# Three-term query products from the second head on, one-hots that read their numbers from PSUM in groups of four tokens, and ten dots a head

## The reference

```
q = (h @ w_q).reshape(B, S, 8 heads, 2, 128)              # query
s = einsum(q, keys)                                       # 128 scores per half, head and token
s_top, i_top = top_k(s, 16)                               # per half
cand = s_top[..., 0, :, None] + s_top[..., 1, None, :]    # 256 candidates
best, pos = top_k(cand, 16); gate = softmax(best)         # 16 experts per head and token
act = gelu(u_tab[idx] . h)                                # idx out of 128*128 experts
y   = sum over the 8*16 experts of gate * act * v_tab[idx]
```

## Time and profile before

| | |
|---|---|
| median of three runs | 3626.38 us |
| the profiled execution itself | 3628.21 us, its span 3626.4 us |
| PE busy | 3406.7 us (94%) |
| DVE busy | 2795.2 us (77%) |
| POOL busy | 1892.1 us (52%) |
| ACT busy | 1113.5 us (31%) |
| mean DMA rate | 236 GB/s |

### The profile page before, as it was taken

The page is one execution under the profiler, slowest core; times in us unless marked ns, Lnnn a source line. Parts: engine busy times, 40 slices in busy tenths (PEclk is TensorE's granted clock), DMA queues, the critical chain, the costliest instruction groups (busy, mean ns, idle before and its releaser), DMA issues. The chain is left out here.

```text
span 3626.4 us, 53931 instructions
## 1 busy us (share of the span) xinstructions
PE 3406.7 (94%) x20084; PEld 2774.6 (77%) x20084; DVE 2795.2 (77%) x4779; ACT 1113.5 (31%) x1630; POOL 1892.1 (52%) x1128
## 2 busy tenths in 40 slices
PE   5998999889999999999999959899999999999995
PEld 2444888748889999988888834688899998888884
DVE  6672455447999999678888864599999994898987
ACT  0112434212223433333333301222243333333332
POOL 1210000015667666678888700456676657888883
PEclk9988999799999999999999979999999999999998
DMA  7750000036778778799999930577788879999994
GB/s 282 280 186 25 2 2 2 12 149 219 277 277 284 226 263 276 278 365 337 340 342 340 315 122 0 181 258 284 261 262 269 265 240 368 341 337 349 340 337 146
DMA packets 366847, 856.06 MB, mean 236 GB/s; under 512 B 32681, under 2 KB 201105, under 8 KB 358322
## 3 DMA queue, kind: packets, MB, share of 16 engines
q1 hardware_dynamic: 281394, 542.91, 44.2%
q0 software_dynamic: 85248, 310.42, 23.7%
HBM read 750.40 MB, written 102.81 MB: 235 GB/s over the span
## 5 line engine op out<-in xcount | busy, mean ns | idle before, releaser
L1442 PE MATMUL peer_acc<-peer_hhi,peer_uhi 128*128 128x384 f32 x2048 | 703.7, 344 | 7.8 <-POOL peer1same_ulo L1607 4.0
L1442 PE MATMUL peer_acc<-peer_hlo,peer_uhi 128*128 128x384 f32 x2048 | 687.2, 336 | 0.0
L1607 POOL TENSOR_TENSOR peer1same_ulo<-peer_u,peer_uhi 128x1024 fp32r<-128x1024 f32 x128 | 337.5, 2638 | 235.0 <-ACT peer_uhi L1510 232.2
L1607 POOL TENSOR_TENSOR peer0same_ulo<-peer_u,peer_uhi 128x1024 fp32r<-128x1024 f32 x128 | 338.0, 2643 | 233.5 <-ACT peer_uhi L1510 231.2
L1442 PEld LDWEIGHTS peer_acc<-peer_hhi,peer_uhi 128*128 128x128 f32 x2048 | 386.8, 189 | 13.2 <-POOL peer1same_ulo L1607 4.8
L1442 PEld LDWEIGHTS peer_acc<-peer_hlo,peer_uhi 128*128 128x128 f32 x2048 | 386.8, 189 | 3.8 <-issue 3.8
L1629 POOL TENSOR_TENSOR peer1lsame_vlo<-peer1l_v,peer1l_vhi 128x1024 fp32r<-128x1024 f32 x128 | 313.3, 2448 | 83.3 <-ACT peer1l_vhi L1535 81.2
L1629 POOL TENSOR_TENSOR peer0lsame_vlo<-peer0l_v,peer0l_vhi 128x1024 fp32r<-128x1024 f32 x128 | 312.6, 2442 | 84.7 <-ACT peer0l_vhi L1535 82.3
L1506 ACT ACTIVATE peer_gel<-peer_acc 128x384 f32<-128x384 f32 x256 | 125.7, 491 | 745.6 <-PE peer_acc L1442 714.4
L1657 DVE SCALAR_TENSOR_TENSOR peer_acc<-peer_row,peer_p_g,peer_acc 128x1024 f32<-128x1024 f32 x254 | 324.8, 1279 | 35.6 <-DMA peer_row<-in_pe_v,peer_idx 33.1
L1442 PE MATMUL peer_acc<-peer_hhi,peer0same_ulo 128*128 128x384 f32 x1024 | 343.8, 336 | 0.0
(11 more groups left out here) (357 smaller groups left out, 7081.9 us busy)
## 6 DMA issues: line engine op xcount, KB each, us to landing
peer_u<-in_pe_uT SPq DMA_DIRECT2D x256, 512.0 KB
peer0l_v<-in_pe_v SPq DMA_DIRECT2D x128, 512.0 KB
peer1l_v<-in_pe_v SPq DMA_DIRECT2D x128, 512.0 KB
activations<-peer_gel SPq DMA_DIRECT2D x256, 192.0 KB
rw_g<-in_ada POOLq DMA_DIRECT2D x80, 512.0 KB, 5.2
routing<-peer0m_wb SPq DMA_DIRECT2D x24, 1024.0 KB, 8.2
peer0l_wt<-routing SPq DMA_DIRECT2D x64, 384.0 KB
peer0l_gl<-activations SPq DMA_DIRECT2D x128, 192.0 KB
```

Of the source, the lines that this page charges most:

```text
L1442: mm = pe.matmul(ub[e % 2][:, 0:SD], a, h[:, k], start=(n == 0), stop=(n == 3 * KT - 1))
L1607: g.tensor_tensor(ulo[:, q].rearrange("p k e -> p (k e)"), u[:, q].rearrange("p k e -> p (k e)"), uhi[:, e % NH].bitcast(F32).rearrange("p ...
```

## The change

1. `query(n)` for n > 0 is a three-term product of 24 matmuls per half: whi*hhi + whi*hlo + wlo*hhi. The weights of head n + 1 are rounded by ACT in two instructions of 1024 elements a partition (`round_query`), in its steps 7n + 2 and 7n + 4, behind `tile_step`. POOL subtracts in two instructions (`low_query`), in its steps 7n + 3 and 7n + 5, behind `low_u` and ahead of the fetches. `whi` lies over `hT`, `wlo` over `wq`. `hhi` and `hlo` are made for 512 columns where there were 384.
2. The list of numbers 0 to 127 (`iota`) is copied to PSUM once, and the one-hots read it there. Groups are of 4 tokens (G = 4), two for each of the 48 tiles; each has its own waits and its own ACT copy.
3. HEAD_DOTS is 10. The 12 dots of a layer that this takes from six heads go to the blocks (57 there, where there were 45).
4. Buffers are laid elsewhere: `pf`, `hot_i` and the rows of the last layer norm.

```diff
-HEAD_DOTS = 12
+HEAD_DOTS = 10
...
-        G = 8
+        G = 4
         GROUPS = P // G
+        A_TILE = GROUPS // BLOCK_TILES
...
+        whi, wlo = over("whi", [P, 2, KT, 2 * P], F32R), over("wlo", [P, 2, KT, 2 * P], F32R)
...
+        iota_p = four[3][:, 0:P]
...
                 def query(n):
                     pe.wait_ge(w_loaded[n % 2], 32 * (n // 2) + 32)
+                    if n > 0:
+                        pe.wait_ge(wlo_made, 2 * n)
                     for s in range(2):
+                        cs = slice(s * P, (s + 1) * P)
                         if n > 0:
                             pe.wait_ge(q_taken, 2 * n + (s - 1))
                         for k in range(KT):
-                            mm = pe.matmul(qb[s], wq[:, n % 2, k, s * P:(s + 1) * P], hT[:, k], start=(k == 0), stop=(k == KT - 1))
+                            if n == 0:
+                                mm = pe.matmul(qb[s], wq[:, 0, k, cs], hT[:, k], start=(k == 0), stop=(k == KT - 1))
+                            else:
+                                pe.matmul(qb[s], whi[:, n % 2, k, cs], hhi[:, k], start=(k == 0), stop=False)
+                                pe.matmul(qb[s], whi[:, n % 2, k, cs], hlo[:, k], start=False, stop=False)
+                                mm = pe.matmul(qb[s], wlo[:, n % 2, k, cs], hhi[:, k], start=False, stop=(k == KT - 1))
                         mm.then_inc(q_done, 1)
...
                     if AT_BLOCKS <= e < AT_LAST:
-                        spread_group(e - AT_BLOCKS)
+                        for n in range(A_TILE * (e - AT_BLOCKS), A_TILE * (e - AT_BLOCKS + 1)):
+                            spread_group(n)
...
+                def round_query(n, half):
+                    ks = slice(half * KT // 2, (half + 1) * KT // 2)
+                    if half == 0:
+                        act.wait_ge(w_loaded[n % 2], 32 * (n // 2) + 32)
+                        act.wait_ge(q_done, 2 * n)
+                        if n <= 2:
+                            act.wait_ge(hlo_made, KT)
+                    a.activation(whi[:, n % 2, ks].rearrange("p k e -> p (k e)"), wq[:, n % 2, ks].rearrange("p k e -> p (k e)"),
+                                 ACT.Copy).then_inc(whi_made, 1)
...
                     tile_step(e)
                     if n < HEADS and r == 0:
                         take_scores(n)
+                    if n + 1 < HEADS and r in (2, 4):
+                        round_query(n + 1, r // 2 - 1)
...
+                def low_query(n, half):
+                    ks = slice(half * KT // 2, (half + 1) * KT // 2)
+                    pool.wait_ge(whi_made, 2 * (n - 1) + (half + 1))
+                    g.tensor_tensor(wlo[:, n % 2, ks].rearrange("p k e -> p (k e)"), wq[:, n % 2, ks].rearrange("p k e -> p (k e)"),
+                                    whi[:, n % 2, ks].bitcast(F32).rearrange("p k e -> p (k e)"), ALU.subtract).then_inc(wlo_made, 1)
...
                 for e in range(ET):
                     low_u(e)
+                    n, r = divmod(e - 1, HEAD_TILES)
+                    if 0 <= n < HEADS - 1 and r in (2, 4):
+                        low_query(n + 1, r // 2 - 1)
                     if e >= HEAD_TILES + 2:
...
-                iota = const["iota"][:]
+                v.tensor_copy(iota_p, const["iota"][:]).then_inc(iota_made, 1)
+                dve.wait_ge(iota_made, 1)
                 dve.wait_ge(slotT_made, 3)
                 for n in range(DT * GROUPS):
                     if n >= 2:
                         dve.wait_ge(spread_done, n - 1)
-                    v.tensor_tensor(hot_j[n % 2], iota.unsqueeze(1).to_broadcast([P, G, P]), spread(slotT[:, 2, n * G:(n + 1) * G], P),
+                    v.tensor_tensor(hot_j[n % 2], iota_p.unsqueeze(1).to_broadcast([P, G, P]), spread(slotT[:, 2, n * G:(n + 1) * G], P),
                                     ALU.is_equal).then_inc(j_made, 1)
                     for q in range(n * G, (n + 1) * G):
-                        ins = v.tensor_scalar(hot_i[:, n % 2, q % G], iota, slotT[:, 1, q:q + 1], slotT[:, 0, q:q + 1], ALU.is_equal,
+                        ins = v.tensor_scalar(hot_i[:, n % 2, q % G], iota_p, slotT[:, 1, q:q + 1], slotT[:, 0, q:q + 1], ALU.is_equal,
                                               ALU.mult)
                     ins.then_inc(i_made, 1)
```

More of the change, by code:

```diff
@@ L1034, in _ @@
             if load_norm is not None:
[L1035 removed]
+                load_norm(sp, rows_loaded, kept)
             if x is not None:
@@ L1277, in phase_peer @@
         gate_g, p_g = arena("gate_g", [P, SLOTS]), arena("p_g", [P, SLOTS])
-        same = Arena(nc, arena.prefix + "same", arena.offset, arena.end)
+        same, ending = Arena(nc, arena.prefix + "same", arena.offset, arena.end), Arena(nc, arena.prefix + "n", arena.offset, arena.end)
+        norm = dict(x=x_sb, **{n: ending(n, [P, D]) for n in ("gate", "g_row", "b_row")})
         u, ulo = arena("u", [P, NU, KT, P]), same("ulo", [P, NU, KT, P], F32R)
@@ L1283, in phase_peer @@
         early = Arena(nc, arena.prefix + "a", shared, arena.end)
+        over = Arena(nc, arena.prefix + "aover", shared, arena.end)
         hT, wq = early("hT", [P, KT, S]), early("wq", [P, 2, KT, 2 * P])
+        whi, wlo = over("whi", [P, 2, KT, 2 * P], F32R), over("wlo", [P, 2, KT, 2 * P], F32R)
         keyT, qT = early("keyT", [P, 2, 2, P]), early("qT", [P, 2, 2, S])
@@ L1299, in phase_peer @@
         wb = middle("wb", [P, 2, P, P // 2])
-        hot_i = middle("hot_i", [P, 2, G, P])
-        hot_j = [kept[n][:].rearrange("p (g q) -> p g q", q=P) for n in ("gate", "g_row")]
+        hot_i = kept["b_row"][:].rearrange("p (b g q) -> p b g q", b=2, q=P)
+        hot_j = [kept[n][:, 0:G * P].rearrange("p (g q) -> p g q", q=P) for n in ("gate", "g_row")]
         late = Arena(nc, arena.prefix + "l", shared, arena.end)
@@ L1307, in phase_peer @@
         vhi = late("vhi", [P, NH, D], F32R)
-        phi, plo, pf = late("phi", [P, NH, SD], F32R), late("plo", [P, NH, SD], F32R), late("pf", [P, NH, SD])
+        phi, plo = late("phi", [P, NH, SD], F32R), late("plo", [P, NH, SD], F32R)
+        pf = [kept[n][:, 0:SD] for n in ("gate", "g_row", "b_row")]
+        assert len(pf) == NH
         acc = ctx.enter_context(nc.psum_tensor(f"{name}_acc", [P, TT, D], F32))
@@ L1314, in phase_peer @@
         qb, sb = four[0:2], [b.rearrange("p (t k) -> p t k", k=P) for b in four[2:4]]
-        hb = [acc[:, b].rearrange("p (t i) -> p t i", i=P) for b in range(2)]
+        hb = [b.rearrange("p (t i) -> p t i", i=P) for b in four[0:2]]
+        iota_p = four[3][:, 0:P]
         x_turned, h_made, hhi_made, hlo_made = sem("x_turned"), sem("h_made"), sem("hhi"), sem("hlo")
@@ L1324, in phase_peer @@
         uhi_made, ulo_made, act_done, gel_made = sem("uhi"), sem("ulo"), sem("act_done"), sem("gel")
+        whi_made, wlo_made, iota_made = sem("whi"), sem("wlo"), sem("iota")
         j_made, i_made, spread_done, taken = sem("hot_j"), sem("hot_i"), sem("spread"), sem("taken")
@@ L1563, in _ @@
                     if AT_BLOCKS <= e < AT_LAST:
-                        take_group(e - AT_BLOCKS)
+                        for q in range(A_TILE * (e - AT_BLOCKS), A_TILE * (e - AT_BLOCKS + 1)):
+                            take_group(q)
                     if e == AT_LAST:
@@ L1758, in _ @@
                     n_rows += 1
+                dve.wait_ge(spread_done, DT * GROUPS)
                 weigh(0)
@@ L1768, in _ @@
                 assert n_dots[0] == n_rows == SLOTS
-        phase_mixer_out(nc, const, Arena(nc, arena.prefix + "o", shared, arena.end), kept, name + "o", y_rows=acc, out=dst)
+        phase_mixer_out(nc, const, Arena(nc, arena.prefix + "o", shared, arena.end), norm, name + "o", y_rows=acc, out=dst)
 def hybrid_trunk(nc, x, xT, ada, ln_g, ln_b, cols_in, const_in, heads_in, scan_in, rw_w_rkv, rw_w0, rw_w1, rw_w2, rw_a1, rw_a2,
@@ L1805, in hybrid_trunk @@
     kept = dict(x=keep("x", [P, TT, D]), **{n: keep(n, [P, D]) for n in ("gate", "g_row", "b_row")})
-    norm_loads = lambda layer, which: lambda sp, loaded: load_norm_rows(sp, kept, layer, which, mod_rows, ln_g[layer, which],
-                                                                        ln_b[layer, which], loaded)
+    norm_loads = lambda layer, which: lambda sp, loaded, into: load_norm_rows(sp, into, layer, which, mod_rows, ln_g[layer, which],
+                                                                              ln_b[layer, which], loaded)
     phase_mixer_out(nc, const, late("out0", rwa.offset), kept, "out0", y_rows=rw["g"], w_out=rw_w_o[0], x=x,
@@ L1811, in hybrid_trunk @@
     pea = late("peer", fixed.offset)
-    pe_t = dict(hhi=pea("hhi", [P, KT, S - P], F32R), hlo=pea("hlo", [P, KT, S - P], F32R))
+    pe_t = dict(hhi=pea("hhi", [P, KT, S], F32R), hlo=pea("hlo", [P, KT, S], F32R))
     E = pe_v.shape[0] // DEPTH
```

24 lines of the change are left out of this document (12 added, 12 removed).

## The result

The changed kernel takes 3735.5 us (median of 4 runs, 3731.9 to 3739.1) against 3627.0 us for the kernel before (4 runs): ratio 1.030 [1.028, 1.033], so 3.0% slower. Its profiled execution took 3731.85 us with a span of 3729.8 us, 103.4 us more than the span of before.

The account below looks back on a forecast made before the run. PE was taken to set the heads and V stage, with DVE next and 7.6 us of the blocks lost to something else. 3628.2 - 39.8 (queries) + 131.4 (stalls) + 78.4 (clock) - 35 (one-hots) = 3763 us; range 3675 to 3815.

Parts of the forecast that it names:

- Queries: Heads: half a query as 48 fp32r matmuls takes 10.89 us against 13.73 a head; -39.8 us over 7 heads, 2 layers.
- The stalls: Heads: `low_query` waits for `whi` in POOL's queue, `ulo` comes late, PE idles 3.4 to 5.7 us; +131.4 us.
- rival 4: Stalls in the heads: DVE keeps the shared port and holds POOL up; +20 us, 3783, counted in the forecast's range.
- The clock: Heads, behind each of 28 stalls: PE's clock falls to 1.2 GHz, costing 2.8 us each; +78.4 us.
- Rival 1: Heads: the stalls come without the clock's fall, heads of 52 us; 3685 us, chance 0.10.
- Blocks: Blocks: one-hots reading PSUM no longer wait for POOL, tiles of 6.0 us; -35 us for two layers.
- Errata and port: Blocks: by the skill's cycle costs a PSUM one-hot is 131 ns dearer, 0.39 us, DVE's tile 5.7 us, still PE's.
- Rivals 2 and 3: 2: POOL's lead covers the wait, 3553 us, chance 0.11; 3: blocks' one-hots still wait for POOL, 3798 us, chance 0.07.
- Costs taken as nothing: `hhi`/`hlo` for 512 columns, moved buffers, waits on `spread_done` and `iota_made`, half-size ACT copies: no cost counted.
- Ten dots: Heads: DVE's 43.09 us less 2 dots of 1.14 is 40.8, under the shorter head's 41.9.

Follow-up runs that it names:

- the fourth experiment: The changed kernel with 24 extra, unused matmuls of 384 columns ahead of PE's waits for `ulo` of tiles 7n+4 and 7n+6: 3683.1 us, ratio 1.017.
- eighth experiment: The best version (both roundings earlier, 3540.8 us) with the first v-table rows fetched at most two a step from POOL's step 115: 3543.8 us, ratio 0.979.

## Why the prediction was right, step by step

The forecast was 3763 us, 0.7% above the 3735.5 measured.

- **Queries.** Said -39.8. The last interval of each head went from 17.89 to 15.11 us: 2.78 each, -39.0 for 14.
- **The stalls.** Said 14 a layer, 131.4 us, behind tiles 7n + 3 and 7n + 5. Measured 14 a layer, 133.6 us. Heads 2 to 6 were said to have 5.7 and 4.5 and had 5.65 and 4.41; head 1, 3.4 and 4.5, had 3.26 and 4.41. Head 0 had 4.2 and 4.6 where 3.4 was said for each. POOL's rows of that place (in the kernel after) show why: its first two `ulo` take 5.67 us together where two take 4.8, and its second `wlo` and `ulo` 6.1. Across the first of them DVE's sum of the candidates' scores (L1733) runs for 3.30 us, where it takes 1.22 to 1.29 in 14 of its 16 places.

```profile
827.24 5.67 POOL L1637 TENSOR_TENSOR peer0same_ulo<-peer_u,peer_uhi 128x1024 fp32r<-128x1024 f32 x2
839.06 2.79 POOL L1643 TENSOR_TENSOR peer0aover_wlo<-peer0a_wq,peer0aover_whi 128x1024 fp32r<-128x1024 f32 x1 [6.15 <-ACT peer0aover_whi L1548]
841.81 3.32 POOL L1637 TENSOR_TENSOR peer0same_ulo<-peer_u,peer_uhi 128x1024 fp32r<-128x1024 f32 x1
```

That is rival 4 (DVE holds POOL up), at 0.8 and 1.2 us; it came true in head 0 alone, some 4 us of the 20 it was priced at. That the wait for `whi` is the cause is shown by moving it alone (3554.8 us) and removing it (3540.8).
- **The clock: the term that was mis-sized.** Said 2.8 us a stall, 78.4 in all. Heads grew by 152.5 us; with the queries' 39.0 back and the stalls' 133.6 off, 57.9 is left, 2.07 each. Counting the matmuls that follow over 0.18 us apart behind each of the 28 stalls gives 57.9 as well: there are 9 to 21 of them, costing 1.5 to 3.0 us. I had priced it from one place, 17 slow matmuls, at the long end of what the stalls showed. Keeping PE at work took 51 us off the heads, with stalls that were a little longer: so the mechanism is shown by an experiment, and about this size with it. Rival 1 (3685) is out: the time lies 50 us over it.
- **Blocks.** Said 6.0 us a tile, -35. Measured 5.96 for every tile, -38.5. No `hot_i` over 0.407 us, `ulo` down from 2643 to 2436 ns in the mean. A `hot_i` follows the next at 0.319 us, said 0.33. That the gain comes with PSUM is shown by the list put back into SBUF.
- **Errata and port.** The Trainium skill, "SBUF — State Buffer", section "Who interferes with whom", says that a DVE instruction contends with GpSimd in the two-port modes or when two of its inputs are in SBUF, and otherwise not. The rows agree: from PSUM no `hot_i` was over 0.407 us and no `hot_j` over 0.692, from SBUF 58 of 768 and 40 of 192 were over 0.8. The figure that the prediction worked out from the Trainium skill, "VectorE: DVE Perf Modes", its section on the TRN2 errata (131 ns dearer from PSUM, an estimate), is not borne out: 0.319 against 0.257 us from start to start is 62 ns.
- **Rivals 2 and 3** are out by the stages: heads of 56 us, not 42, and tiles of 5.96 us, not 6.4. **Costs taken as nothing** were nothing: the stages around the blocks did not move (34.3, and 70.1 to 70.5 us).
- **Ten dots.** DVE "would allow" the shorter head for the wrong reason. I took the 43.09 us of the earlier trace rows less two dots; twelve fit as well.

The sum of what was measured: -39.0 + 133.6 + 57.9 - 38.5 = +114.0, and about -10 from the stretches with unchanged code. Against the forecast's +134.8 the clock's term makes 20.5 of the difference.

## What to carry to other kernels

In a queue that keeps its order, an instruction costs what everything behind it has to wait for, not its own length. Before adding one, ask when its input is ready, and put it where that has been true for some time: here the same instructions gave +3.0% in one place, -1.9% with one of them two steps later, and -2.2% with both where their data were ready. And an idle time of an engine in the rows isn't the only sign of a wait: an instruction whose mean is far above its shortest is waiting too, and moving its operand out of the shared memory, or its place, brings that back.

## What the runs showed of the hardware

- PE's clock: behind idle times of 3.3 to 5.7 us it was at the 1.2 GHz level (granted 0.50), and 384-column matmuls followed at 0.32 in place of 0.173 us for 9 to 21 of them. Behind three of the 28 stalls (3.26, 4.23 and 4.41 us idle) it fell only after PE had started again, and the first matmul or two still followed at the faster pace. The same idle time of 3.85 us was followed by 15, 18, 19 and 21 such matmuls in four places of the kernels before and after. With idle times of up to 1.5 us in the fourth experiment it stayed at 1.00.
- A one-hot of 128 columns follows the next at 0.319 us with its list in PSUM, 0.257 in SBUF, though the profile draws it at 0.401 us.
- The same DVE sum of 1024 elements on SBUF operands took 3.97 us where it fell beside a POOL instruction and 1.23 where it did not, and which of the two held was moved by edits elsewhere. The 58 slow `hot_i` from SBUF ended 0.08 to 0.09 us behind a POOL subtraction; from PSUM 382 started while one ran, and none took over 0.407 us. So a DVE that the rows show busy for 41.4 of 41.85 us had room for two dots of 1.2 us more.
- The queues moved 415 GB/s in the stretch in which the U tiles came late (eighth experiment), at a DMA share of 1.03.
